# Three model blocks on one core: the order of the five engines' work at each change of stage, and pairs of slabs opened three blocks apart

## The reference

```
block 1: h = rmsnorm(x); a, b, z, q, f, i, g, mc, mr = split(h @ w_in)       # 9 parts of 1024
  y_conv = (silu(layernorm(conv31(a * sigmoid(b)))) * silu(z)) @ w_conv_out
  y_rec  = (rmsnorm(hgrn2(q, f, i)) * silu(g)) @ w_rec_out                   # gated linear recurrence
  x = rmsnorm(x + (sigmoid(mc) * y_conv + sigmoid(mr) * y_rec) @ w_out)
block 2: n = rmsnorm(x) @ w_in_2 -> attention over a band, gated conv3, spatial gating unit
  x = x + grouprmsnorm(concat) @ w_out_2;  x = x + relu(rmsnorm(x) @ w_up)^2 @ w_down;  x = rmsnorm(x)
block 3: u = x @ w_in_3 -> 4 heads of mLSTM (conv4, input and forget gates), mean pools of windows 2, 4, 8, 16
  y_p = einsum(pooled, w_pool) * scale;  x = layernorm(ALPHA x + concat(y_m, y_p) @ w_out_3)
  x = layernorm(ALPHA x + relu(x @ w_ff1)^2 @ w_ff2)
```

## Time and profile before

| what | us |
|---|---|
| median of 3 runs | 4136.83 |
| profiled execution | 4137.56 |
| its span | 4136.2 |
| TensorE busy | 3803.0 |
| VectorE, ScalarE, GpSimd busy | 1757.2, 1138.4, 1042.8 |
| mean granted clock of TensorE | 0.957 |

### The profile page before, as it was taken

The page is one execution under the profiler, slowest core; times in us unless marked ns, Lnnn a source line. Parts: engine busy times, 40 slices in busy tenths (PEclk is TensorE's granted clock), DMA queues, the critical chain, the costliest instruction groups (busy, mean ns, idle before and its releaser), DMA issues.

```text
span 4136.2 us, 41632 instructions
## 1 busy us (share of the span) xinstructions
PE 3803.0 (92%) x17820; PEld 3102.3 (75%) x17820; DVE 1757.2 (42%) x1954; ACT 1138.4 (28%) x1414; POOL 1042.8 (25%) x416
## 2 busy tenths in 40 slices
PE   7999999999979989999989999998998969999995
PEld 6988887877767767666778888876676758888884
DVE  4565535999833343223332222224456252222225
ACT  4444432212231223443221112113322131111112
POOL 3343331222233431001332222222111422222221
PEclk9999999999989989999999999998999979999997
DMA  2000011111232221000211111112001201111111
GB/s 95 29 23 26 26 61 57 51 51 46 72 112 82 92 81 49 31 22 27 79 41 46 46 46 46 46 51 74 31 31 31 82 26 46 46 46 46 49 48 46
DMA packets 57927, 210.97 MB, mean 51 GB/s; under 512 B 6416, under 2 KB 6544, under 8 KB 57616
## 3 DMA queue, kind: packets, MB, share of 16 engines
q1 hardware_dynamic: 57744, 208.31, 15.2%
HBM read 183.12 MB, written 25.17 MB: 50 GB/s over the span
## 4 chain that ended last, share of the span: by engine, by line
PE 73%; DVE 19%; ACT 4%; issue 2%; POOL 1%; DMA 1%; SPq 0%; ACTq 0%; DVEq 0%; POOLq 0%
PE psum L400 62%; DVE Cb L1711 8%; PE psum L482 2%; PE psum L729 1%; PE psum L715 1%; PE psum L455 1%; PE psum L440 1%; DVE hl L1551 1%; DVE t L2009 1%; PE psum L751 1%; POOL wl L2270 0%; DVE hdl L2011 0%; POOL accc L2365 0%; DVE fb L1645 0%; ACT t L1417 0%
## 5 line engine op out<-in xcount | busy, mean ns | idle before, releaser
L2270 POOL TENSOR_TENSOR wl<-raw,wh 128x1024 fp32r<-128x1024 f32 x283 | 704.7, 2492 | 2580.5 <-ACT wh L958 2580.5
L400 PE MATMUL psum<-hh,wh 128*128 128x512 f32 (+2 forms) x3760 | 1175.9, 399 | 128.4 <-DVE hl L1551 46.7
L400 PE MATMUL psum<-hh,wl 128*128 128x512 f32 (+2 forms) x3760 | 1126.7, 385 | 0.0
L400 PE MATMUL psum<-hl,wh 128*128 128x512 f32 (+2 forms) x3760 | 1119.3, 383 | 0.0
L400 PEld LDWEIGHTS psum<-hh,wh 128*128 128x128 f32 x3760 | 680.3, 194 | 282.6 <-issue 125.8
L400 PEld LDWEIGHTS psum<-hh,wl 128*128 128x128 f32 x3760 | 711.0, 193 | 138.9
L400 PEld LDWEIGHTS psum<-hl,wh 128*128 128x128 f32 x3760 | 706.8, 192 | 136.3
L958 ACT ACTIVATE wh<-raw 128x1024 fp32r<-128x1024 f32 x283 | 298.3, 1054 | 909.2 <-PE psum L400 902.0
L1711 DVE SCALAR_TENSOR_TENSOR Cb<-av,vec,Cb 128x1024 f32<-128x1024 f32 x240 | 372.6, 1553 | 8.3
L2017 DVE TENSOR_TENSOR B<-B,psum 128x1024 f32<-128x1024 f32 x128 | 156.3, 1221 | 504.0 <-PE psum L400 504.0
L400 PE MATMUL psum<-hdh,wh 128*128 128x512 f32 x1024 | 324.9, 398 | 13.1 <-DVE hdl L2011 13.1
(11 more groups left out here) (362 smaller groups left out, 3027.8 us busy)
## 6 DMA issues: line engine op xcount, KB each, us to landing
raw<-in_wts SPq DMA_DIRECT2D x283, 512.0 KB, 3.5
keep_x<-B SPq DMA_DIRECT2D x16, 512.0 KB, 4.1
t<-keep_x SPq DMA_DIRECT2D x15, 512.0 KB, 3.3
X<-in_xin SPq DMA_DIRECT2D x8, 520.0 KB, 5.2
keep_sz<-tmp SPq DMA_DIRECT2D x8, 512.0 KB, 2.9
tmp<-keep_sz SPq DMA_DIRECT2D x8, 512.0 KB, 5.0
av<-keep_gr SPq DMA_DIRECT2D x8, 512.0 KB, 3.5
av<-keep_gc SPq DMA_DIRECT2D x8, 512.0 KB, 3.3
```

The costliest lines, as they stand in the source:

```text
L400: ins = pe.matmul(out, w, x[:, k, c0:c0 + width], start=first and n == 0, stop=final and n == 2)
L2270: gp.tensor_tensor(wl[:, s, :], raw[:, s, :], fp(wh[:, s, :]), SUB).then_inc(*c.lo.tick(i))
```

## The change

It moves instructions; the work itself stays. Two loads of ScalarE's function tables fall away, and eight instructions change engine: seven additions of squares `accc<-accc,tmp` and one `hl` (tile 5 of the stage OUT2) go from GpSimd to VectorE.

1. `duo` opens a pair three blocks apart in place of one (`duo_steps`), on all engines; the second slab's PSUM pair and weights are asked for only where it starts.
2. `last_slab` on ScalarE: in the last slab of the stages ahead of REC, CNV, OUT1, OUT2 and OUT3 the next stage's `high` of a tile comes as soon as TensorE has used the tile before it. VectorE's and GpSimd's `low` follow, VectorE's ahead of that slab's evacuation for tiles 0, 1, 2 and 4 and behind it for tile 6; the `split` of the pair's second slab goes behind.
3. `conv_norm` is cut in two: sums and spread keep their place in GATE_C, with other pauses, and `conv_gate` (scaling, silu, product with `sz`) runs in the REC pair. SP loads `sz` then.
4. Two-layer stages: the first down slab takes three blocks of either half first and the fourth blocks last (`DOWN_FIRST`).
5. GATES3: the gates' chain on ScalarE and VectorE comes behind the first evacuation of head 0 and its taps. In the heads `pause(4)` becomes `pause(7)`, and the yields around P and si stand differently.
6. POOL3 takes its groups in the order 3, 2, 1, 0, each group's product behind the next slab, the last in the OUT3 pair; OUT3 takes its tiles as in `CAT_ORDER`, OUT2 as in `MIX_ORDER`.
7. ScalarE no longer waits for the whole norm before SGU's first gelu.

The diff, cut to its core:

```diff
+DOWN_REST = tuple((e, k) for e in range(2) for k in range(4))
+DOWN_FIRST = ((0, 0), (0, 1), (0, 2), (1, 0), (1, 1), (1, 2), (0, 3), (1, 3))
...
+def duo_steps(lag=3):
+
+    for n in range(KT + lag):
+        if n < KT:
+            yield 0, n
+        if n >= lag:
+            yield 1, n - lag
...
+    def on_pool(ver, k):
+
+        return k in GP_TILES and (ver, k) != ("mix", 5)
...
-    MIX_LATE = (3, 6, 7, 4)
-    OUT2_ORDER = (0, 1, 2, 3, 6, 7, 4, 5)
+    MIX_ORDER = (0, 1, 2, 3, 4, 6, 7, 5)
+    CAT_ORDER = (0, 1, 2, 7, 6, 5, 3, 4)
+    POOLS = (3, 2, 1, 0)
...
-            prs = [grab(pairs, (i + e, 0), untils[e]) for e in range(2)]
-            hds = [grab(head, (i,), lead) if lead else None, None]
-            for n in range(KT + 1):
-                for e in range(2):
-                    if not 0 <= n - e < KT:
-                        continue
-                    k = order[n - e]
-                    if n == e:
-                        pe.wait_ge(*c.lo(i + e))
-                    if e == 0:
-                        pe.wait_ge(*low_done(ver, k))
-                    ins = three(prs[e], hds[e], i + e, k, k, n == e, n - e == KT - 1, hh, hl, META)
-                    if n - e == KT - 1:
-                        ins.then_inc(*c.gemm.tick(i + e, 0))
-                    side.turn()
+            prs, hds = [None, None], [None, None]
+            for e, n in duo_steps():
+                k = order[n]
+                if n == 0:
+                    prs[e] = grab(pairs, (i + e, 0), untils[e])
+                    if e == 0 and lead:
+                        hds[0] = grab(head, (i,), lead)
+                    pe.wait_ge(*c.lo(i + e))
+                if e == 0:
+                    pe.wait_ge(*low_done(ver, k))
+                ins = three(prs[e], hds[e], i + e, k, k, n == 0, n == KT - 1, hh, hl, META)
+                if n == KT - 1:
+                    ins.then_inc(*c.gemm.tick(i + e, 0))
+                side.turn()
...
+                    prs = [None, None]
+                    for e, k in DOWN_FIRST if j == 0 else DOWN_REST:
+                        if k == 0:
+                            prs[e] = grab(pairs, (i, e), c.ev_v("dn", base, g, 2 * j + e))
+                            if e == 0:
+                                pe.wait_ge(*c.lo(i))
+                        if j == 0 and e == 0:
+                            pe.wait_ge(*c.ml_dve("lo", base, 4 * g + k))
+                        ins = three(prs[e], None, i, k, 4 * e + k, k == 0, k == 3, xh, xl, 0)
+                        if k == 3:
...
-            yield from pause(4)
+            yield from pause(7)
...
+        def pool_product(g):
...
+        def last_pool():
+            yield from pause(4)
+            pool_product(POOLS[3])
+
+        for n, g in enumerate(POOLS):
+            gemm(POOL3 + n, c.ev("pl", g), last=(n == 3))
+            if n == 1:
+                pe.wait_ge(*c.loaded("w_pool"))
+            if n:
+                pool_product(POOLS[n - 1])
+        side.finish(job)
+        side.add(last_pool())
+        duo(OUT3, "cat", [c.ev_v("x3", 0), c.ev_v("x3", 1)], order=CAT_ORDER)
+        side.drain()
         for m in range(2, 8):
...
+        def last_slab(i, ver, tiles):
+
+            split(i + 1)
+            for k in range(KT - 1):
+                side.turn()
+                if k in tiles:
+                    high(ver, k, *tiles[k])
+            side.turn()
...
-            slab(i, last=(m == 7))
+            if m < 7:
+                slab(i)
+            else:
+                last_slab(i, "rec", {k: (O[:, k, :], c.cv_dve("o", k)) for k in range(KT)})
+                side.finish(job)
+                split(i + 2)
...
-        for k in range(KT):
-            high("rec", k, O[:, k, :], c.cv_dve("o", k))
+        high("rec", 7, O[:, 7, :], c.cv_dve("o", 7))
+        side.add(conv_gate())
         duo(REC)
-        for m in range(2, 8):
-            slab(REC + m, last=(m == 7))
-        side.finish(job)
-        for k in range(KT):
-            high("cnv", k, Cb[:, k, :], c.cv_dve("cf", k))
+        for m in range(2, 7):
+            slab(REC + m)
...
-            slab(i + 2, last=(m == 1))
+            if m == 0:
+                slab(i + 2)
+            else:
+                side.drain()
+                last_slab(i + 2, "mix", {k: (MX[:, k, :], mixed(k)) for k in (0, 1, 2, 3, 4, 6)})
...
+        def gates_log():
+            se.wait_ge(*c.gt_dve("f"))
...
+
+        def gates_exp():
+            se.wait_ge(*c.gt_dve("si"))
+            se.activation(f_, f_, EXP).then_inc(*c.gt_act.tick("si"))
+            se.wait_ge(*c.gt_dve("em"))
...
+                if h == 0:
+                    gates_exp() if n else gates_log()
...
+            i = POOL3 + n
+            if n == 2:
+                pooled(POOLS[0])
+            if n < 3:
+                slab(i)
+            else:
+                pooled(POOLS[1])
+                last_slab(i, "cat", {0: (Y[:, 0, :], c.ms_dve("y", 0, 1)), 1: (Y[:, 1, :], c.ms_dve("y", 1, 1)),
+                                     2: (Y[:, 2, :], c.ms_dve("y", 2, 1)), 6: (Y[:, 6, :], c.ev("py", 2, 1))})
...
+        split(OUT3 + 1)
+        high("cat", 7, Y[:, 7, :], c.ev("py", 3, 1))
+        pooled(POOLS[2])
+        high("cat", 5, Y[:, 5, :], c.ev("py", 1, 1))
+        high("cat", 3, Y[:, 3, :], c.ms_dve("y", 3, 1))
+        pooled(POOLS[3])
+        high("cat", 4, Y[:, 4, :], c.ev("py", 0, 1))
...
+            def add(k):
+                ve.wait_ge(*c.sq("cs", k))
+                if k > 1:
+                    ve.wait_ge(*c.acc_v("cs", k - 1))
+                ve.tensor_tensor(accc[:, :], accc[:, :], tmp[:, (23 + k) % 3, :], ADD).then_inc(*c.acc_v.tick("cs", k))
...
-                ve.wait_ge(*c.loaded("sz", k))
-                ve.tensor_tensor(Cb[:, k, :], Cb[:, k, :], tmp[:, (31 + k) % 3, :], MUL).then_inc(*c.cv_dve.tick("cf", k))
+            for k in range(9):
+                if k < 8:
+                    ve.tensor_tensor(Cb[:, k, :], Cb[:, k, :], R, MUL).then_inc(*c.cv_dve.tick("cr", k))
+                if k:
+                    ve.wait_ge(*c.cv_act("silu", k - 1))
+                    ve.wait_ge(*c.loaded("sz", k - 1))
+                    ve.tensor_tensor(Cb[:, k - 1, :], Cb[:, k - 1, :], tmp[:, (30 + k) % 3, :],
+                                     MUL).then_inc(*c.cv_dve.tick("cf", k - 1))
+                yield
...
+        side.add(conv_gate())
         side.turn(16)
         for m in range(8):
-            if m >= 2:
+            if 2 <= m < 7:
                 side.turn(8)
+            if m == 7:
+                side.drain()
+                for k in (0, 1, 2, 4):
+                    low("cnv", k, Cb[:, k, :])
             ve.wait_ge(*c.gemm(REC + m, 0))
...
+        for n in range(3):
+            side.turn(8)
+            pooled(n)
+        for k in (0, 1, 2):
+            side.turn(2)
+            low("cat", k, Y[:, k, :])
...
-            low("cat", k, Y[:, k, :])
+        low("cat", 6, Y[:, 6, :])
+        pooled(3)
+        low("cat", 4, Y[:, 4, :])
 
 
...
+        def stage(first, ver, src):
+            low(ver, 3, src[:, 3, :])
+            low(ver, 5, src[:, 5, :])
+            split(first + 1)
+            low(ver, 7, src[:, 7, :])
+            duo(first)
...
+        def conv_gate():
             for k in range(8):
                 if k < 3:
-                    sp.wait_ge(*c.acc_p("cs", 5 + k))
+                    sp.wait_ge(*c.acc_v("cs", 5 + k))
                 else:
...
         sp.wait_ge(*c.stored("gc", 7))
+        side.add(conv_gate())
         branch(REC, "gr", lambda m: GR[m], lambda m: c.ev_v("rec", m) if m >= 0 else c.stored("gc", 5))
```

More of the change, by code:

```diff
@@ L805, in mlp @@
                     i = base + 8 * g + 4 + j
[L806 to L814, removed]
+                    prs = [None, None]
[8 more added lines that the diff above has]
+                        if k == 3:
+                            ins.then_inc(*c.gemm.tick(i, e))
         duo(MLP2, "ff2", [c.ev("up", MLP2, 0), c.ev("up", MLP2, 1)])
@@ L1240, in scalar @@
             if m >= 2:
-                slab(OUT1 + m, last=(m == 7))
+                slab(OUT1 + m)
+            if m == 7:
+                split(OUT1 + 9)
             se.wait_ge(*c.ev_v("out", m))
@@ L1380, in scalar @@
                 side.add(tile_norm(0))
-        side.drain()
-        for k in (0, 1, 2):
-            high("mix", k, MX[:, k, :], mixed(k))
+        split(OUT2 + 1)
         side.add(tile_norm(1))
         side.turn()
-        for k in MIX_LATE:
-            high("mix", k, MX[:, k, :], mixed(k))
+        high("mix", 7, MX[:, 7, :], mixed(7))
         duo(OUT2)
@@ L1393, in scalar @@
             if m >= 2:
-                slab(OUT2 + m, last=(m == 7))
+                slab(OUT2 + m)
+            if m == 7:
+                split(OUT2 + 9)
             se.wait_ge(*c.ev_v("x2", m))
@@ L1536, in scalar @@
         for m in range(2, 8):
-            slab(OUT3 + m, last=(m == 7))
+            slab(OUT3 + m)
```

(52 more changed lines are left out.)

301 lines of the change are left out of this document (126 added, 175 removed).

## The result

The changed kernel takes 4043.28 us (median of 4 runs, 4041.07 to 4044.21), the kernel before 4137.44 (4 runs): a ratio of 0.9771, 95% interval 0.9754 to 0.9788. The forecast was 4052, the range 4025 to 4092. The profiled span is 4041.8 us, 94.4 less.

What follows compares the result with a forecast made beforehand. TensorE, busy 92% of the span, bounds the kernel, so its idle 333 us and the clock behind it count. Gains of 97.5 less 12.2 for the wider gap give 85.3 off 4137.56: some 4052 us, range 4025 to 4092.

Steps and rivals of the forecast that it cites:

- Into REC: GATE_C into REC: roundings come first, VectorE's evacuation of REC's first slab becomes the late one; +18 us (14 to 22).
- CNV, OUT1, OUT2: Pairs of these stages: tiles rounded in the slab ahead remove most of the excess; +7, +9 and +12 us.
- SGU: SGU: its second evacuation no longer waits for the whole norm, but the pair wants tiles earlier; +4 us (-1 to 6).
- Two-layer stages: MLP2 and MLP3: three blocks of the other half cover the sixteen waits for `hdl`; +13 us (9 to 16).
- GATES3: GATES3 to HEADS3's fourth slab: `pre` comes ahead of the logs, leaving a new 4.6 us weights wait; +6 (0 to 10).
- Heads: Heads 0 to 2: regrouped yields give VectorE two to three blocks more before `h` is used; +15 us (8 to 19).
- POOL3 and OUT3: POOL3 into OUT3: each pool product hides behind a slab, about 3.5 us of low clock stays; +13.5 us (9 to 16).
- The wider gap: Four pairs keeping old roundings want tiles two blocks earlier: -7.2 us, and -5 for low clock behind stalls.
- A: Rival, starvation: all pairs run short for three blocks and drop the clock, 17 us more, 4069; chance 0.12.
- B: Rival, VectorE's queue: REC's evacuation up to 10 later, pooled means 5, heads keep 5; 4072 us; chance 0.18.
- C: Rival, slower than before: ScalarE conversions in the last slab wait for sources and hold what follows; about 4168; chance 0.05.
- D: Rival, no change: tiles come earlier but each pair then waits for weights; gain under 8 us; chance 0.03.

Runs made afterwards that it cites:

- The seventh experiment: Changed kernel with conv_gate spread wider in the REC pair, ScalarE's silu and SP's loads paced to match: 4033.68 us.
- the third experiment: Changed kernel with the tiles of CNV and OUT1 rounded behind the last slab of the stage ahead again: 4063.51 us.
- the first: Changed kernel with all pairs opened one block apart again in place of three: 4043.53 us, ratio 0.9770 to the kernel before.
- the fifth experiment: Changed kernel with the old pause of four turns in the heads in place of seven, regrouped yields kept: 4055.58 us.
- the best version with P together: Changed kernel with conv_gate spread wider, weights ahead of GATES3's exponentials and gaps set per pair, P products in one turn: 4015.34 us.
- the best version: Changed kernel with conv_gate spread wider, weights ahead of GATES3's exponentials, gaps set per pair and P products in two turns: 4015.00 us.

## Why the prediction was right, point by point

*What bounds the kernel.* Right: TensorE's instructions are the same, and idle time and clock account for all of the gain. Of the signs named ahead these came: no wait above 2 us ahead of CNV, OUT1 and OUT2, none for `hdl`, `h` under 1 in heads 0 to 2, idle time of 266.6 for 270, and a wait of 1.5 for the second spread.

*Into REC.* The size was right, 20.7 for 18. The new wait was there, 6.27 us for some 7. Its releaser was only half named, as the chain of waits after shows:

```profile
1193.38 1.05 ACT wh L979
...
1194.50 5.60 POOL wl L2358
...
1200.23 4.94 PE psum L418 x13
```

VectorE's evacuation ended at 1199.01, as forecast (1201), but the weights ended at 1200.09: ScalarE had rounded them behind six silu, and GpSimd's `wl` took 5.60 beside VectorE in place of 2.43. The first `sz` cost VectorE 1.8 us, not the whole of the load's time. The seventh experiment took both queues away. Which part of the change gave how much of the 20.7 was not taken apart.

*CNV, OUT1, OUT2.* Right in mechanism and size. For CNV and OUT1 the third experiment showed the rounding in the last slab as the cause, and the first that the gap is what the second weights need: with it the feared wait behind GpSimd's two tiles stayed out, and with a gap of one it came. For OUT2, which also takes its tiles in another order, the rounding as the cause is read from the same pattern and was not tested.

*SGU.* Right, 3.9 for 4. The gap costs 2 us of it.

*Two-layer stages.* The mechanism was right, the term was mis-sized: 17.7 for 13, outside its range of 9 to 16. The step "fourteen short ones may keep 0.14 each" failed, they kept nothing. The two long waits were worth 4.1 us each (17.7 less 9.5, by two), clock included, and either of two edits removes them, of which I had priced one.

*GATES3.* Right, 7.0 for 6: 33.19 us for the forecast 33, and the forecast wait of 4.6 for the weights was 4.59, behind k's silu.

*Heads.* Right in the wait, wrong in what removes it, too high in size: 10.4 for 15. The prediction gave the blocks that cover `h` to the regrouped yields; the fifth experiment gives them to the pause, three blocks longer. In heads 0 to 2 the waits for `h` fell from 13.3 to 2.6 us, but the clock did not come back with them. Before, each of the three waits had 6.8 us of half clock behind it; after, there are stretches of 3.4 without such a wait.

*POOL3 and OUT3.* Right in size. No experiment took it apart. Head 3's wait for `h` is gone, and the low clock that was to stay behind it, some 3.5 us, is there at another place: two half-clock stretches of 3.4 us in the OUT3 pair, where the waits are 2.95 for GpSimd's `hl` and 2.17 for the last pooled means.

*The wider gap.* -9.3 for -12.2 with the low clock, right in sign and place. The term for the clock was mis-sized. A little of it is there, inside the 9.3: the first slab behind MLP2's pair took 12.80 us at a clock of 0.87, 1.6 more than before,

```profile
2080.17:2092.97 12.80, 12.80 (x48) 10.29 (x49) 6.14 (x4) 3.03 (x3) 1.48 (x1) 0.87 0.12 41
```

but it took 11.22 at full clock in the seventh experiment's kernel, with the same gap, and 12.79 in the first's, with the old one. So the gap isn't shown to cost it.

*How near it came.* The 9 us between forecast and result are a sum of errors of both signs: 4.7 from the two-layer stages, 2.9 from gap and clock and 2.7 from REC, against 4.6 too many for the heads. Part of the nearness is luck.

*Rivals.* A held in part: the pairs starve, but for 9.3 us and not 29. B's queue was there, as in the forecast, but not its price: the evacuation came at 1199 and not ten later, and the heads kept 2.6 us of their wait and not 5. C did not come: conversions in the last slab held nothing back. D neither. The drain that the Trainium skill, "ScalarE: Activation LUTs", section "What ACT_TABLE_LOAD costs", adds to each switch isn't in the trace after either: the table load ahead of the last evacuation of GATE_C ended at 1174.20 and the activation began at 1174.21.

## What to carry to other kernels

At a change of stage, look which instructions of the in-order engines need only what is long there, and put them into the last slab ahead; here that gave 7 to 11 us each at CNV, OUT1 and OUT2. A parameter that helps one place by time and costs another (the gap) shows no effect as a whole: match the two traces instruction by instruction, and set it for each place. Before a small difference is believed, look whether it is one half-clock stretch more or less. After each wait is gone look at what now stands between the same two instructions, for the next 7 to 8 us lay in the queue beside it at REC and behind GATES3.

## What was not expected of the hardware

In the heads TensorE's granted clock fell to half (0.51) from 2931.00 to 2934.40 while TensorE was busy for 3.40 of 3.40 us, and the wait ahead of it, 10 us earlier, was 0.86. Kernels whose heads are the same code showed two to six such stretches, and 245.1 to 249.8 us for the same slabs. It is not the heads alone. From the end of SGU to the start of OUT2 the changed kernel and its variants run the same code. That part in the changed kernel, in the best version with P together, and in the best version:

```profile
1525.84:1939.36 413.52, 390.27 (x1929) 283.84 (x1928) 131.85 (x298) 162.78 (x305) 46.67 (x19) 0.99 0.10 31
```

```profile
1511.90:1922.50 410.60, 387.14 (x1929) 281.18 (x1928) 131.68 (x306) 161.72 (x304) 45.74 (x19) 1.00 0.10 31
```

```profile
1510.28:1925.65 415.37, 391.92 (x1930) 284.91 (x1929) 131.80 (x298) 162.89 (x305) 46.95 (x19) 0.99 0.10 31
```

They hold two, none and three half-clock stretches of 3.4 us, for the same work. What tips the clock, the small matmuls or the place in time, was not found.
